# First layer's output projection and residual norm in segments of 512, 512 and 256 tokens

## What is computed

```
for layer in range(2):
    with_ctx = layer < 1
    ...
    o_l = concatenate([a_l, b_l, c_l, d_l], axis=-1) @ w_out     # output projection
    x_l = x_l + mod_l[2] * rms_norm(o_l, norm_post_mix)          # residual norm
    f_l = conv_ffn(modulate(rms_norm(x_l, norm_pre_ffn), mod_l[3], mod_l[4]), ...)
    x_l = x_l + mod_l[5] * rms_norm(f_l, norm_post_ffn)
    if with_ctx: ...                                             # the same for the 256 context rows
```

## Time and profile before

| | us |
|---|---|
| median of 3 runs | 4517.78 |
| lowest, highest | 4515.36, 4520.21 |
| profiled execution | 4514.93 |
| its span, first to last instruction | 4513.1 |

### The profile page before, as it was taken

One profiled execution on the slowest core, in us unless ns is written; L12 is line 12 of the kernel. 1 busy time (PEld: TensorE's weight loads), 2 busy tenths in 40 slices (PEclk: granted clock), 3 DMA queues, 4 the chain that ended last, 5 costly groups with the idle time before them and its releaser, 6 DMA issues. The chain is left out here.

```text
span 4513.1 us, 81348 instructions
## 1 busy us (share of the span) xinstructions
PE 3889.6 (86%) x33432; PEld 3142.0 (70%) x33432; DVE 2089.7 (46%) x2906; ACT 1342.9 (30%) x1881; POOL 1075.9 (24%) x848
## 2 busy tenths in 40 slices
PE   6999559678887999999997999559678788999997
PEld 3888435456766888888885888345557677888885
DVE  3464755565547332233225344755555564332334
ACT  5121333233333321221225222433343334222223
POOL 1000510004521332332232000510015413243343
PEclk9999679799988999999998999679889999999999
DMA  5444130010012111111111334130010021111112
GB/s 192 159 158 159 54 115 1 18 38 3 4 62 92 52 33 39 35 37 37 37 52 51 111 126 149 53 113 1 18 39 4 31 84 61 48 43 54 46 47 93
DMA packets 73757, 287.93 MB, mean 64 GB/s; under 512 B 8080, under 2 KB 13456, under 8 KB 68496
## 3 DMA queue, kind: packets, MB, share of 16 engines
q1 hardware_dynamic: 57360, 203.63, 13.2%
q10 hardware_dynamic: 16128, 80.49, 4.9%
HBM read 228.77 MB, written 47.45 MB: 61 GB/s over the span
## 5 line engine op out<-in xcount | busy, mean ns | idle before, releaser
L3222 DVE SCALAR_TENSOR_TENSOR y<-ps,taps,y 128x1023 f32<-128x1023 f32 (+1 forms) x132 | 134.1, 1016 | 863.5 <-DVEq L3220 857.0
L496 PE MATMUL ps<-h_hi,wu_hi 128*128 128x512 f32 x1680 | 460.0, 371 | 9.5 <-PEq L3122 9.5
L496 PE MATMUL ps<-h_hi,wu_raw_rest 128*128 128x512 f32 x1680 | 459.4, 371 | 0.0
L496 PE MATMUL ps<-h_whole_rest,wu_hi 128*128 128x512 f32 x1680 | 459.1, 371 | 0.0
L3314 POOL TENSOR_TENSOR wu_raw_rest<-wu_raw,wu_hi 128x1024 fp32r<-128x1024 f32 x84 | 201.5, 2398 | 1020.9 <-POOLq L3313 1020.9
L496 PE MATMUL ps<-h_hi,w_hi 128*128 128x512 f32 (+1 forms) x1200 | 313.4, 365 | 35.8 <-PEq L492 35.8
L496 PEld LDWEIGHTS ps<-h_hi,wu_hi 128*128 128x128 f32 x1680 | 294.4, 188 | 66.0 <-issue 9.8
L496 PEld LDWEIGHTS ps<-h_hi,wu_raw_rest 128*128 128x128 f32 x1680 | 294.7, 188 | 56.3
L496 PEld LDWEIGHTS ps<-h_whole_rest,wu_hi 128*128 128x128 f32 x1680 | 294.2, 188 | 56.3
L496 PE MATMUL ps<-h_hi,w_raw_rest 128*128 128x512 f32 (+1 forms) x1200 | 311.9, 364 | 0.0
L496 PE MATMUL ps<-h_whole_rest,w_hi 128*128 128x512 f32 (+1 forms) x1200 | 311.4, 364 | 0.0
(11 more groups left out here) (393 smaller groups left out, 7858.8 us busy)
## 6 DMA issues: line engine op xcount, KB each, us to landing
wu_raw<-in_w_up_dram SPq DMA_DIRECT2D x88, 512.0 KB, 3.2
w_raw<-in_w_in_dram SPq DMA_DIRECT2D x54, 512.0 KB, 4.6
ada_w<-in_ada_rest_dram ACTq DMA_DIRECT2D x27, 1024.0 KB, 6.8
rows<-rows ACTq DMA_DIRECT2D x42, 640.0 KB, 4.7
wd_raw<-in_w_down_dram SPq DMA_DIRECT2D x40, 512.0 KB, 4.3
ada_w<-in_ada_rest_dram ACTq DMA_DIRECT2D x27, 512.0 KB, 4.9
h_whole<-rows SPq DMA_DIRECT2D x20, 640.0 KB, 7.3
wd_raw<-in_w_out_dram SPq DMA_DIRECT2D x18, 512.0 KB, 3.4
```

Of the source, the lines that this page charges most:

```text
L496: mm = pe.matmul(ps[:, lo:lo + width], w[a][:, t, :], rhs[b][:, t, lo:lo + width], start=(t == 0 and i == 0), stop=(t == n_k - 1 and i == 2))
L3222: dve.scalar_tensor_tensor(y[:, s, lo + 1:hi], ps[s][:, lo:hi - 1], k.taps[:, s, 0:1], y[:, s, lo + 1:hi], ALU.mult, ALU.add).then_inc(own ...
```

## The change

The first layer's segments become 512, 512 and 256 tokens; the second layer keeps 512, 256 and 256. So the first layer has 24 products instead of 32 and 16 weight loads instead of 20. The second segment's moved rows are now 512 wide and no longer fit the odd buffer: tiles 0 to 3 lie in it (`odd_low`), tiles 4 to 7 lie in the rounded inputs' place (`hi_plain`, the first 512 tokens of `k.hi`, which the first segment's products have finished with). Since `upper` of segment 0 writes there later, it waits for tiles 4 to 7 from the fourth added tile of segment 1 on. The factor of the last segment lies in a free half of `acc1`.

```diff
     def factor2_of(self, s):
         w = self.segs[s][1]
+        if self.segs[1][1] == 512:
+            return self.acc1[:, 0, 256:256 + w] if s == 2 else self.r2[:, 0:w]
         at = 256 * (s % 2)
         return self.r2[:, at:at + w]
...
     def upper(self, act, s, t):
         h_done, hi_done = self.mark("h_done"), self.mark("hi_done")
         act.wait_ge(h_done.sem, h_done.at(8 * s + t + 1))
+        if s == 0 and self.segs[1][1] == 512 and t >= KD // 2:
+            x_added = self.mark("x_added")
+            act.wait_ge(x_added.sem, x_added.at(8 + KD // 2))
...
+        hi_at = k.nc.sbuf_base - 4 * KD * T
         f = k.xT
-        segs = [(0, 512)] + [(lo, 256) for lo in range(512, n, 256)]
+        segs = [(0, 512), (512, 512), (1024, n - 1024)] if n > SEQ else [(0, 512)] + [(lo, 256) for lo in range(512, n, 256)]
+        wide = segs[1][1] == 512
...
-        mixed = [over("mixed_even", [P, KD, 512], at_g), over("mixed_odd", [P, KD, 256], at_g + 16384)]
+        mixed_even, mixed_odd = over("mixed_even", [P, KD, 512], at_g), over("mixed_odd", [P, KD, 256], at_g + 16384)
+        odd_low = over("odd_low", [P, KD // 2, 512], at_g + 16384)
+
+        hi_plain = over("hi_plain", [P, KD, T], hi_at)
+
+        def mixed(s, t):
+            w = segs[s][1]
+            if s % 2 == 0:
+                return mixed_even[:, t, 0:w]
+            if not wide:
+                return mixed_odd[:, t, 0:w]
+            return odd_low[:, t, :] if t < KD // 2 else hi_plain[:, t, 0:512]
...
-        ref = Refresh(k, segs, orders, 2, 3, 4, lambda s, t: mixed[s % 2][:, t, 0:segs[s][1]],
+        ref = Refresh(k, segs, orders, 2, 3, 4, mixed,
...
-                    act.activation(mixed[s % 2][:, t, 0:segs[s][1]], place_of(i), ACT.Copy).then_inc(evicted.sem, 1)
+                    act.activation(mixed(s, t), place_of(i), ACT.Copy).then_inc(evicted.sem, 1)
```

## The result

| | before | changed |
|---|---|---|
| median of 4 runs each, us | 4517.51 | 4489.66 |
| lowest, highest | 4515.36, 4520.21 | 4486.27, 4490.53 |
| profiled execution (span) | 4514.93 (4513.1) | 4490.53 (4488.6) |

The ratio of the two is 0.9941, 95% interval 0.9928 to 0.9955: the change is faster by 27.9 us in the medians. The sign and the mechanism were right. The size was not: the sum was forecast as -18.5 and measured as -27.9, and much of what follows is about these 9.4 us.

A forecast was written before the change was run, and what follows sets the result against it. The prediction took a loop of VectorE and ScalarE, not TensorE, to bound the output projection. M2's -18.0 and the tail's -0.5 summed to -18.5 us: 4496.4 for the profiled execution, 4499.3 for the median, range 4491 to 4508 (87%).

The forecast's parts named there:

- The start of the phase and the level: First layer's output projection: products 0 to 7 start unchanged; profiled time 4514.9 becomes 4496.4, median 4517.8 becomes 4499.3 us.
- M3: ScalarE's first instruction of the first layer's ConvFFN, 1492.14 us before; forecast near 1473.6, its shift being the whole gain.
- M1: Last rounding of the second segment, 1382.10 us before; forecast at 1394.1, 12.0 us late.
- M1 to the L2834 of product 2: Start of the last segment: two closing sums, two products and the factors; forecast to stay at 10.2 us.
- The turns of the last segment: From product 2's L2834 to the last: 29.79 us from the second layer plus 6.2 for wider rows, 36.0 us.
- M2: L2834 for the phase's last product, 1458.27 us before; forecast at 1440.3, a move of -18.0 us.
- The tail: M2 to M3, 33.87 us before; forecast change -0.5 us, bounds -1.5 to +3.
- the first rival: TensorE's clock stays low behind M2 and through the first FFN tile: up to +25 us, time 4524; chance 4%.
- The new wait: In upper(), for the second segment's fourth added tile before the first segment's tile 4 is rounded: claimed to cost nothing.
- Collisions as a rival: GpSimd's eight copies in the two last segments slow wider VectorE instructions, 3.0 us each: time 4517, no change; chance 6%.
- TensorE bound in the second segment: Third rival: ScalarE's work hides under TensorE, M1 at 1389.7, 4.4 us better, time 4495; in the range, no separate chance.
- the loop: Output-projection turns: VectorE and ScalarE wait on each other and set the pace, 7.17 or 6.30 us a product before.

The follow-up runs named there:

- four later comparisons: Kernel before and changed kernel, both unchanged, run side by side again: medians 4508.0 to 4511.0 us before, 4485.2 to 4490.4 changed, gains 17.9 to 24.1.
- the variant with the later pair: Changed kernel, but GpSimd rounds the second up-projection tile only when the last product is moved out: 4487.4 us against 4487.6, ratio to the kernel before 0.9952.
- the variant with the earlier work: Changed kernel with norm factors and earlier segments' row work one product earlier, both layers: 4479.3 us, ratio to the kernel before 0.9930.

## Why the prediction was right and wrong, step by step

- **The start of the phase and the level** is the step that failed. "Products 0 to 7 start where they did" and "a shift of M3 is the whole change of the time" put the gain onto one profiled execution, and "4517.8, for which I say 4499.3", with 2.5 us for the median of three runs, put it onto three runs. The same kernel's medians were 4508.0 to 4511.0 in four later comparisons, and its phase started anywhere from 1288.8 to 1297.8. Of the 9.4 us that the first comparison gained beyond the forecast, 5.7 lie ahead of the phase, 1.2 behind M3 and 3.5 in how the two profiled executions lie to their medians, less 0.9 by which the phase gained less than forecast (to rounding). The range left out the spread of the stretches that the change doesn't touch. It is also narrower than the bounds that it lists: added up, these reach 10.9 us below the forecast, to 4488.4.
- **M1** was forecast 12.0 late within the phase and came 11.6 late. The turn of product 2 was 7.12 us, and TensorE's longest wait in the last product 1.3 us where some 4 were expected.
- **M1 to the L2834 of product 2** was taken at 10.2, and was 10.98 or 9.3, by the clock at the two sums. The forecast had no term for that clock.
- **The turns of the last segment**, 36.0 forecast from the second layer's pattern, took 36.24 (1398.97 to 1435.21). The prediction calls them six, but from the L2834 of product 2 to that of product 7 there are five distances, in the pattern too, so the sum is not touched. The longest was 10.2, with the meeting; the others were 9.5, 8.1, 6.9 and 1.6. Two of them are outside the "turns of 8 to 11 us" that it named as a sign, though their sum was right.
- **M2** within the phase moved by -17.4, forecast -18.0.
- **The tail** moved by -0.2, forecast -0.5. TensorE's wait before it was 10.0 us (9 estimated), and the clock behind it 0.92: it did not stay low, so the first rival fell.
- **The new wait** in `upper` cost nothing. Its first use for tile 4 is at this row of ScalarE, which waited for `scale_x` and not for the added rows:

```profile
1423.43 0.73 ACT L2952 ACTIVATE h_hi<-h_whole,mods 128x512 fp32r<-128x512 f32 x1 [0.63 <-DVE h_whole L2942]
```

- **Collisions as a rival** fell: one meeting cost 2.2 us, none of the others in these two segments over 0.9 for an instruction or a pair. By the Trainium skill, page "GPSIMD Engine Reference", section "Specifications", GpSimd and VectorE contend over SBUF when VectorE's instruction has two inputs there. The rows agree, and the variant with the later pair shows what a meeting costs.
- **TensorE bound in the second segment**, the third rival, was half right: TensorE was busy for 45.3 of 46.9 us there, but M1 came 11.6 us late, as the loop had it, and not the 7.6 of this rival.
- **Behind M3** the 1.2 us of the second layer's ConvFFN were not foreseen.

**What stays open.** The first comparison's gain is 7 us above the 20.8 of the others. All four runs of the kernel before were high there, those of the changed kernel beside it were not. With only 5 of 104 later runs as high, four chance draws are a poor account, but no later comparison showed the gap again. The later ones ran on four different chips, and the chip of the first is not on record. So a condition of that chip or that time, which touches one program and not the other, remains possible and unshown. Nor is it known what decides the clock's level at the two sums, what "issue" stands for, or why the last 1.2 us go with the program.

## What to carry to other kernels

Forecast the change from marks inside the phase that it touches: the phase's length repeated within 0.4 us in the kernel before and within 2.0 in the changed one, while its start moved by 9. Then put it onto a level from as many runs as there are, with the spread of the untouched stretches in the range, since three runs that agree within 5 us were nearly 9 us from where the same kernel ran later. Before widening a segment, read which engine is idle at its start: wider segments were worth 16.5 us of the phase here, and giving the idle engine its work one product earlier another 10 us of the time, in both layers together.

## What the hardware showed

- A stretch of thousands of small matmuls varies in idle time that no wait explains, 14.1 to 20.3 us of 227 in the sixteen profiles, and its length from the mixer's first matmul to the phase by up to 9.1 us.
- Two pairs of fp32 sums took 1.02 us each at a granted clock of 1.00, or 1.78 and 1.91 at 0.52, at the same place of the same program, and moved the end of the phase by 1.7 us.
- VectorE lost 2.1 to 2.2 us each time that one of its two-input instructions or pairs met GpSimd's subtraction of 128x1024 in the changed kernel and its variant with the later pair, whether GpSimd took 2.3 or 3.5 us. Where one pair of instructions met GpSimd's copy and its subtraction together, in the variant with the earlier work, it lost 2.9 (4.27 for 1.41).
- Leaving out 82 of 130 recorded matmuls in a stretch that VectorE keeps busy for 22 us brought TensorE's granted clock from 0.85 to 0.63 and its busy time from 26.3 to 18.3 us, but the stretch from 28.3 to only 25.9.
